# First attention of a two-block network in pairs of heads: row groups, column groups, one instruction for bias and maximum

## The chip, the cores and the metric

The kernel runs on one core of a Trainium2 chip. The metric is the device time of one execution in microseconds, the median of the runs shown. The core has a matrix engine (TensorE, PE in the rows, its weight loads PEld), a vector engine (DVE), an activation engine (ACT), GpSimd (POOL) and a sync engine (SP) that issues the weight transfers.

## The reference

Two transformer blocks in fp32 over 256 tokens of width 1024. The change touches the attention of the first block alone: eight sliding-window heads (window 128, two key/value heads, a learned sink per head) and eight heads that see all earlier tokens, each of width 64, each with a bias by distance.

```python
s = einsum(q, k) * HEAD_DIM ** -0.5 + bias          # masked: -inf
m = maximum(max(s), sink)                           # no sink in the second eight
p = exp(s - m); p = p / (sum(p) + exp(sink - m))
o = einsum(p, v)                                    # 64 columns per head
merged = sigmoid(ga) * (oa @ w_branch_a) + sigmoid(gb) * (ob @ w_branch_b)
```

The products with weights that surround it (`gate` = ga and gb, `bra` and `brb` = the two branches) use weights that arrive as fp32 and are split on the chip into a high part (`whi`) and a low part (`wlo`), so that each 128x128 tile takes three matmuls of 256 columns.

## The kernel before, in words

Each engine has its program written out by hand; the order in the source is the order on the engine, and semaphores tie them together. Weights come in chunks of 128 x 1024 (512 KB), in `raw`. For a chunk that is multiplied, ACT writes `whi` (L1138) and DVE writes `wlo` (L1518). For a chunk of the modulation weights (`ada`), DVE multiplies and adds two pieces of 512 columns (`ada_piece`, L1538 for a first part, L1541 for later ones, L1547 sums at the end of four). Scores of a head are fp32 matmuls, which the trace shows as two instructions each.

The stage of interest runs over `i = 0..17`. In step `i` TensorE does the scores of head `i` (`scores1`, L734 and L735, 64 rows of the array, into bank `A[i % 2]`), the 24 matmuls of `gate{i}` (L614 to L616), the three transposes of head `i-1` (L745) and the values of head `i-2` (`values1`, L759 and L760, 64 columns of the array, into `A[3]`). After steps 4, 8, 12 and 16 it also turns a modulation sum (`mod_sum`, L660).

DVE in step `i` does `shifts1(i)`: scaled score plus bias into `sc1` (L1680, L1681), two maxima (L1687, L1688), for heads with a sink the sink's maximum (L1691); then the `ada` piece of the step, the reciprocal (L1697 and L1699 with a sink, L1702 without), `splits(gate i)`, which is the low half of the chunk that `gate{i+1}` opens with (L1518), after odd steps the affine step that makes a sigmoid of the tanh (L1720), and the low half of a pair's output (L1728). ACT does the exponentials (L1257, L1258, L1260), the high half of a chunk that lies two gates ahead, the tanh (L1268), the copy of the transposed weights (L1275) and the high half of the output (L1279). GpSimd multiplies the exponentials by the reciprocal (L2129, L2130). `p1`, `sc1` and `pT1` hold two heads each.

The low half that `gate{i+1}` needs is thus made on DVE behind the shift, the `ada` piece and the reciprocal of head `i`, all of which wait for the scores of head `i`.

Of the kernel before, what the change touches and what calls it, by code (L numbers as in the profile page):

```python
# [14 lines left out]
P = 128  # L15
# [5 lines left out]
HD = 64  # L21
# [368 lines left out]
def build_program(nc, xT, metaT, vecs, consts, bands, bias_oh, bias_rows, wstream, scratch, outT):  # L390
# [6 lines left out]
    with ctx:  # L397
# [136 lines left out]
        ada_sets += [(flat(sc1[:, :, :])[:, 0:4 * P], flat(p1[:, :, :])[:, 0:4 * P])]  # L534
# [55 lines left out]
        def tensor_program(e):  # L590
# [146 lines left out]
            def transposes1(i):
# [5 lines left out]
                for j in range(3):  # L743
                    to = (j + 1) % 3
                    m = e.transpose(A[2][:, to * P:(to + 1) * P], p1[:, i % 2, j * P:(j + 1) * P], ident)  # L745
                m.then_inc(transposed1, 1)

            def values1(i):
                h, b, half = heads[i], i % 2, i % 2
                vv = lambda kt: vtok[:, kt, h["v"]:h["v"] + HD]  # L750
                o = A[3][half * HD:(half + 1) * HD, :]
                if i == 0:
# [3 lines left out]
                elif not half:  # L756
                    e.wait_ge(o_lo, i // 2)
                e.wait_ge(pT1_done, i + 1)
                e.matmul(o[:, 0:SEQ], vv(0), pT1[:, b, 0:SEQ], start=True, stop=False, skip_group_check=True)  # L759
                e.matmul(o[:, P:SEQ], vv(1), pT1[:, b, SEQ:384], start=False, stop=True, skip_group_check=True).then_inc(valued1, 1)  # L760
# [9 lines left out]
            for i in range(HEADS1 + 2):  # L770
                if i < HEADS1:
                    scores1(i)
                    if i % 2 == 0:
                        gate_out = pair(f"gate{i}")
                    gemm(f"gate{i}", [gate_out[:, t, 0:SEQ] for t in range(2)], src1, k0=4 * (i % 2), ktotal=KT)
                else:
                    branch_a(i - HEADS1)
                if 1 <= i <= HEADS1:
                    transposes1(i - 1)
                if i >= 2:  # L780
                    values1(i - 2)
                if i in HEAD_MODS:
                    mod_sum(HEAD_MODS[i], int(HEAD_MODS[i][3:]))
# [343 lines left out]
        def scalar_program(e):  # L1127
# [103 lines left out]
            def qk_copy(i):  # L1231
# [6 lines left out]
                e.activation(dst, ps[:, :, :, ::-1] if 1 <= ts[0] <= 4 or ts[0] >= 9 else ps, ACT.Copy).then_inc(qk_act, 1)  # L1238
# [13 lines left out]
            def exps1(i):  # L1252
                h, b, st = heads[i], i % 2, stat[:, i % 4, :]
# [1006 lines left out]
```

## Time and profile before

| | |
|---|---|
| median of 3 runs | 1271.12 us (1270.24 to 1271.15) |
| the profiled execution | 1270.07 us, its span 1268.5 us |
| mean granted TensorE clock | 0.997 |
| busy: PE, PEld, DVE, ACT, POOL | 97%, 95%, 69%, 50%, 14% of the span |
| the stage of the change | from 79.5 us (first scores) to about 170.5 us (last values) |

A busy PE is modelled from pipelined matmuls; the distance from one start to the next tells more than a duration. Idle time is shown in square brackets with what ended it.

### The profile page before, as it was taken

The page shows a single profiled execution, that of the slowest core. Times are in us where ns is not written, and L with a number is a line of the kernel's source. Part 1 is how long each engine was busy: PE and PEld are TensorE (multiplying, and loading weights), DVE is VectorE, ACT ScalarE, POOL GpSimd, SP SyncE. Part 2 cuts the span into 40 slices and gives each one's busy share as a digit, 9 for nine tenths or more (in the row PEclk, how much of TensorE's full clock was granted, in tenths as well). Part 3 has the DMA queues.
Part 4 walks back from the last instruction along what each step waited for, and adds up shares of the span by engine and source line. Part 5 has one row for each costly group of instructions (what it writes and reads, how often), then busy time and mean ns, then how long its engine had stood idle before and what let it go on. Part 6 is the DMA issues. An engine that isn't in the chain of part 4 may idle for free.

```text
span 1268.5 us, 23765 instructions
## 1 busy us (share of the span) xinstructions
PE 1230.6 (97%) x9924; PEld 1202.7 (95%) x9924; DVE 879.5 (69%) x1239; ACT 633.5 (50%) x986; POOL 177.8 (14%) x177
## 2 busy tenths in 40 slices
PE   4999999999999999999999999999999999999997
PEld 3998899999999999999899999999999997999997
DVE  7789889877566766655666666666666786766654
ACT  5545545766444444543544444445444466545531
POOL 2015424000132000012200001220000231000021
PEclk9999999999999999999999999999999999999999
DMA  8976564666655555555355555455656532655650
GB/s 325 324 305 207 203 250 161 242 248 248 212 158 166 178 186 168 180 170 181 100 175 184 174 185 166 166 173 192 196 178 208 183 116 68 215 181 186 190 160 34
DMA packets 67570, 239.16 MB, mean 189 GB/s; under 512 B 7366, under 2 KB 9592, under 8 KB 67464
## 3 DMA queue, kind: packets, MB, share of 16 engines
q1 hardware_dynamic: 66872, 235.46, 55.3%
q0 software_dynamic: 592, 2.19, 0.5%
q8 instruction: 78, 1.28, 0.4%
q14 instruction: 28, 0.23, 0.1%
HBM read 236.55 MB, written 1.07 MB: 187 GB/s over the span
## 4 chain that ended last, share of the span: by engine, by line
PE 87%; DVE 6%; ACT 1%; issue 1%; POOL 1%; DVEq 0%; ACTq 0%
PE G L614 26%; PE G L615 26%; PE G L616 26%; DVE sb_wlo L1518 2%; PE A L759 1%; PE A L734 1%; PE A L614 1%; PE A L615 1%; PE A L616 1%; DVE sb_xl L2044 0%; DVE sb_hidf L1607 0%; ACT sb_whi L1138 0%; PE A L745 0%; DVE sb_xl L1583 0%; PE A L1027 0%
## 5 line engine op out<-in xcount | busy, mean ns | idle before, releaser
L1518 DVE TENSOR_TENSOR sb_wlo<-sb_raw,sb_whi 128x1024 fp32r<-128x1024 f32 (+1 forms) x398 | 485.9, 1254 | 80.8 <-ACT sb_whi L1138 80.5
L614 PE MATMUL G<-sb_xh,sb_whi 128*128 128x256 f32 (+2 forms) x1752 | 497.9, 284 | 5.0 <-DVE sb_wlo L1518 2.2
L615 PE MATMUL G<-sb_xl,sb_whi 128*128 128x256 f32 (+2 forms) x1752 | 497.8, 284 | 0.0
L616 PE MATMUL G<-sb_xh,sb_wlo 128*128 128x256 f32 (+2 forms) x1752 | 496.3, 283 | 0.0
L1138 ACT ACTIVATE sb_whi<-sb_raw 128x1024 fp32r<-128x1024 f32 (+1 forms) x398 | 405.0, 1043 | 182.9 <-PE G L616 166.3
L614 PEld LDWEIGHTS G<-sb_xh,sb_whi 128*128 128x128 f32 x1752 | 330.7, 189 | 8.3 <-DVE sb_gu L1846 2.6
L616 PEld LDWEIGHTS G<-sb_xh,sb_wlo 128*128 128x128 f32 x1752 | 330.4, 189 | 0.0
L615 PEld LDWEIGHTS G<-sb_xl,sb_whi 128*128 128x128 f32 x1752 | 330.0, 188 | 0.0
L614 PE MATMUL G<-sb_hh,sb_whi 128*128 128x256 f32 (+1 forms) x1056 | 299.1, 283 | 0.7 <-DVE sb_hh L1738 0.7
L616 PE MATMUL G<-sb_hh,sb_wlo 128*128 128x256 f32 (+1 forms) x1056 | 298.2, 282 | 0.0
L615 PE MATMUL G<-sb_hl,sb_whi 128*128 128x256 f32 (+1 forms) x992 | 280.4, 283 | 0.0
L614 PEld LDWEIGHTS G<-sb_hh,sb_whi 128*128 128x128 f32 x1056 | 198.6, 188 | 1.1 <-issue 0.6
L616 PEld LDWEIGHTS G<-sb_hh,sb_wlo 128*128 128x128 f32 x1056 | 198.6, 188 | 0.0
L615 PEld LDWEIGHTS G<-sb_hl,sb_whi 128*128 128x128 f32 x992 | 186.7, 188 | 0.0
L1364 ACT ACTIVATE sb_gu<-sb_gu 128x272 f32<-128x272 f32 (+1 forms) x88 | 37.4, 425 | 191.6 <-DVE sb_gu L1846 191.3
L1846 DVE TENSOR_TENSOR sb_gu<-G,sb_rstd 128x544 f32<-128x544 f32 (+1 forms) x84 | 59.4, 707 | 60.1 <-PE G L616 60.1
L2086 POOL TENSOR_TENSOR sb_sumsq<-sb_X 128x256 f32<-128x256 f32 (+1 forms) x6 | 3.7, 622 | 651.5 <-DVE sb_X L1576 651.5
L1852 DVE TENSOR_TENSOR sb_hidf<-sb_gu 128x272 f32<-128x272 f32 (+1 forms) x88 | 38.2, 434 | 50.1 <-ACT sb_gu L1364 50.1
L1855 DVE TENSOR_TENSOR sb_hl<-sb_hidf,sb_hh 128x272 fp32r<-128x272 f32 (+1 forms) x88 | 38.1, 434 | 43.2 <-ACT sb_hh L1366 43.2
L1366 ACT ACTIVATE sb_hh<-sb_hidf 128x272 fp32r<-128x272 f32 (+1 forms) x88 | 37.4, 425 | 50.6 <-DVE sb_hidf L1852 50.6
L2091 POOL TENSOR_TENSOR sb_sq<-sb_X 128x256 f32<-128x256 f32 (+1 forms) x41 | 31.5, 767 | 203.7 <-DVE sb_X L1576 203.7
L1576 DVE SCALAR_TENSOR_TENSOR sb_X<-G,sb_X 128x272 f32<-128x272 f32 (+1 forms) x32 | 12.4, 427 | 48.0 <-PE G L616 48.0
(328 smaller groups left out, 1301.2 us busy)
## 6 DMA issues: line engine op xcount, KB each, us to landing
sb_raw<-in_wstream SPq DMA_DIRECT2D x438, 512.0 KB, 4.4
sb_raw<-in_wstream SPq DMA_DIRECT2D x8, 320.0 KB, 6.4
sb_bias<-bias_scratch POOLq DMA_DIRECT2D x1, 2048.0 KB, 16.0
sb_X<-in_xT SPq DMA_DIRECT2D x2, 512.0 KB, 6.4
out_T<-sb_X SPq DMA_DIRECT2D x4, 256.0 KB, 2.7
sb_con<-in_consts SPq DMA_DIRECT2D x1, 601.0 KB, 7.8
sb_band<-in_bands SPq DMA_DIRECT2D x1, 314.0 KB, 4.8
sb_vec<-in_vecs SPq DMA_DIRECT2D x1, 82.5 KB, 2.0
```

The lines of the kernel that those rows point to most:

```text
L614: e.matmul(out, w_h, xs, start=k0 + s.kt == 0, stop=False)
L615: e.matmul(out, w_h, xr, start=False, stop=False)
L616: m = e.matmul(out, w_l, xs, start=False, stop=k0 + s.kt == ktotal - 1)
L734: e.matmul(bank[:, 0:SEQ], q(1), k(SEQ), start=True, stop=True)
L1138: e.activation(whi[:, i % NSPLIT, 0:w], raw[:, c % NRAW, 0:w], ACT.Copy).then_inc(hi_done, 1)
L1364: e.activation(gu[:, b, 0, 0:n], gu[:, b, 0, 0:n], ACT.Silu).then_inc(silu_done, 1)
L1366: e.activation(hh[:, j * n:(j + 1) * n], hidf[:, b, 0:n], ACT.Copy).then_inc(hid_hi, 1)
L1518: e.tensor_tensor(wlo[:, i % NSPLIT, 0:w], raw[:, c % NRAW, 0:w], f(whi[:, i % NSPLIT, 0:w]), ALU.subtract).then_inc(lo_done, 1)
L1846: e.tensor_tensor(gu[:, b, :, 0:n], G[plan.pair[name]][:, :, 0:n], rb, ALU.mult).then_inc(left_dve, 1)
L1852: e.tensor_tensor(hidf[:, b, 0:n], gu[:, b, 0, 0:n], gu[:, b, 1, 0:n], ALU.mult).then_inc(hid_mul, 1)
L1855: e.tensor_tensor(hl[:, sl], hidf[:, b, 0:n], f(hh[:, sl]), ALU.subtract).then_inc(hid_lo, 1)
L2091: e.tensor_tensor(s, src, src, ALU.mult).then_inc(sumsq_done, 1)
```

## The change

- TensorE: the stage runs over pairs `p` of heads (rows 0 to 63 and 64 to 127 of the array, banks `A[0]` and `A[1]`). The scores of a pair stand together, head by head in turn; then the transposes of head `2p-2`, `gate{2p}`, the modulation sum, the transposes of head `2p-1`, `gate{2p+1}`, and the values of the earlier pair, again in turn, in column groups 0 to 63 and 64 to 127.
- DVE: bias, sign and minimum in one `tensor_tensor_reduce` per part (it writes the negative of score plus bias into `p1` and the negative maximum, clamped by the sink, into `stat`). Both heads of a pair are shifted before the first `ada` piece. The scale of 1/8 moves to the copies of the queries. `sc1` is gone, `p1` holds four heads, and the exponential works in place with scale -1.
- The sigmoid's affine step is gone: `(tanh + 1)` is multiplied in where the branch is gated, and the factor 0.5 goes into the copy of the attention's output.

```diff
-            def scores1(i):
+            def scores1(p):
+                pairs = [(heads[2 * p + n], A[n]) for n in range(2)]
...
+                for h, bank in pairs:
+                    e.matmul(bank[:, 0:SEQ], q(h, 1), k(h, SEQ), start=True, stop=True)
+                for h, bank in pairs:
+                    e.matmul(bank[:, SEQ:SEQ + P], q(h, 0), k(h, P), start=True, stop=True).then_inc(scored1, 1)
...
+                e.wait_ge(pT1_done, 2 * p + 2)
+                for n in range(2):
+                    e.matmul(o(n)[:, 0:SEQ], vv(n, 0), pT1[:, n, 0:SEQ], start=True, stop=False, skip_group_check=True)
+                for n in range(2):
+                    m = e.matmul(o(n)[:, P:SEQ], vv(n, 1), pT1[:, n, SEQ:384], start=False, stop=True, skip_group_check=True)
+                m.then_inc(valued1, 1)
...
+            for p in range(HEADS1 // 2 + 1):
+                if p < HEADS1 // 2:
+                    scores1(p)
+                    gate_out = pair(f"gate{2 * p}")
+                if p:
+                    transposes1(2 * p - 2)
+                if p < HEADS1 // 2:
+                    gate_src(2 * p)
+                else:
+                    branch_a(0)
+                if 2 * p in HEAD_MODS:
+                    mod_sum(HEAD_MODS[2 * p], int(HEAD_MODS[2 * p][3:]))
+                if p:
+                    transposes1(2 * p - 1)
+                if p < HEADS1 // 2:
+                    gate_src(2 * p + 1)
+                else:
+                    branch_a(1)
+                if p:
+                    values1(p - 1)
...
-                e.activation(p1[:, b, 0:SEQ], sc1[:, b, 0:SEQ], ACT.Exp, bias=st[:, 0:1], accum_out=st[:, 2:3])
+                e.activation(w[:, 0:SEQ], w[:, 0:SEQ], ACT.Exp, bias=st[:, 0:1], scale=-1.0, accum_out=st[:, 2:3])
...
-                e.scalar_tensor_tensor(sc1[:, b, 0:SEQ], bank[:, 0:SEQ], HD ** -0.5, bias[:, h["bias"], :], ALU.mult, ALU.add)
-                e.tensor_reduce(md[:, 0:1], sc1[:, b, 0:SEQ], AX_X, ALU.max, negate=neg)
+                e.tensor_tensor_reduce(w[:, 0:SEQ], bank[:, 0:SEQ], bias[:, h["bias"], :], -1.0, least, ALU.add, ALU.min, st[:, 0:1])
+                e.tensor_tensor_reduce(w[:, SEQ:384], bank[:, SEQ:384], bias[:, h["bias"], P:SEQ], -1.0, least, ALU.add, ALU.min, st[:, 1:2]).then_inc(sc1_done, 1)
...
+                    shifts1(2 * p)
+                    shifts1(2 * p + 1)
+                    if p:
+                        ada_piece(*ADA_HEADS[2 * p])
+                    recip1(2 * p)
+                    splits(f"gate{2 * p}")
+                    recip1(2 * p + 1)
...
+                    ada_piece(*ADA_HEADS[2 * p + 1])
+                    splits(f"gate{2 * p + 1}")
...
-                        e.tensor_scalar(d, d, 0.5, 0.5, ALU.mult, ALU.add).then_inc(sig_done, 1)
+                e.scalar_tensor_tensor(dst, sig[:, t:t + 2, :], 1.0, G[plan.pair[name]][:, :, 0:SEQ], ALU.add, ALU.mult).then_inc(left_dve, 1)
```

On TensorE before, between two gates, for a head in mid-stage (`A2` takes transposes, `A3` values, `A0` and `A1` scores):

```order
L616 MATMUL G1<-sb_xh,sb_wlo 128x256
L745 MATMUL A2<-sb_con,sb_p1 128x128 [waits weighted1,pT1_done]
L745 MATMUL A2<-sb_con,sb_p1 128x128 x2
L759 MATMUL A3<-sb_pT1,sb_vtok 64x256 [waits pT1_done]
L760 MATMUL A3<-sb_pT1,sb_vtok 64x128
L734 MATMUL A0<-sb_qk 128x256 [waits sc1_done]
L735 MATMUL A0<-sb_qk 128x128
```

The same place after the change, between the two gates that enclose a pair's beginning (line numbers are the changed kernel's):

```order
L763 MATMUL A3<-sb_pT1,sb_vtok 64x256 [waits pT1_done,o_lo]
L763 MATMUL A3<-sb_pT1,sb_vtok 64x256
L765 MATMUL A3<-sb_pT1,sb_vtok 64x128 x2
L736 MATMUL A0<-sb_qk 128x256 [waits sc1_done]
L736 MATMUL A1<-sb_qk 128x256
L738 MATMUL A0<-sb_qk 128x128
L738 MATMUL A1<-sb_qk 128x128
L748 MATMUL A2<-sb_con,sb_p1 128x128 [waits weighted1,pT1_done,left_act]
L748 MATMUL A2<-sb_con,sb_p1 128x128 x2
```

Values and scores of two heads stand side by side, and one head's transposes moved behind the scores; the other head's stand between the two gates.

On DVE before, the work of one head with a sink, up to the low half of the next gate's chunk:

```order
L1680 SCALAR_TENSOR_TENSOR sb_sc1<-A1,sb_bias 128x256
L1681 SCALAR_TENSOR_TENSOR sb_sc1<-A1,sb_bias 128x128
L1687 TENSOR_REDUCE sb_stat<-sb_sc1 128x1
L1688 TENSOR_REDUCE sb_stat<-sb_sc1 128x1
L1691 TENSOR_SCALAR sb_stat<-sb_stat,sb_vec 128x2
L1541 SCALAR_TENSOR_TENSOR sb_gu<-sb_raw,sb_csil,sb_gu 128x512 x2
L1697 TENSOR_TENSOR sb_stat<-sb_stat 128x2
L1699 RECIPROCAL sb_stat<-sb_stat 128x2
L1518 TENSOR_TENSOR sb_wlo<-sb_raw,sb_whi 128x1024
```

The same place after, for a pair with sinks; each `ISA` row with `sb_p1` is a `tensor_tensor_reduce`, the row of one column behind it reads its result out:

```order
L1716 ISA sb_p1,sb_stat<-A0,sb_bias,sb_neg_sinks 128x256 [waits transposed1,scored1]
L1716 ISA sb_stat 128x1
L1717 ISA sb_p1,sb_stat<-A0,sb_bias,sb_neg_sinks 128x128
L1717 ISA sb_stat 128x1
L1716 ISA sb_p1,sb_stat<-A1,sb_bias,sb_neg_sinks 128x256 [waits transposed1,scored1]
L1716 ISA sb_stat 128x1
L1717 ISA sb_p1,sb_stat<-A1,sb_bias,sb_neg_sinks 128x128
L1717 ISA sb_stat 128x1
L1569 SCALAR_TENSOR_TENSOR sb_gu<-sb_raw,sb_csil,sb_gu 128x512 [waits ada_acc,loaded5]
L1569 SCALAR_TENSOR_TENSOR sb_gu<-sb_raw,sb_csil,sb_gu 128x512 [waits ada_acc]
L1723 TENSOR_TENSOR sb_stat<-sb_stat 128x2 [waits sink_done]
L1725 RECIPROCAL sb_stat<-sb_stat 128x2 [waits den_done]
```

Behind these rows comes the low half of the chunk of `gate{2p+1}` (L1546). The shifts of a second head now stand ahead of it.

## Rows read from the trace of the kernel before

**Rows 1.** The page's first part: busy time and share of each engine.
```profile
PE 1230.6 (97%) x9924; PEld 1202.7 (95%) x9924; DVE 879.5 (69%) x1239; ACT 633.5 (50%) x986; POOL 177.8 (14%) x177
```
**Rows 2.** Windows: stretch, length, PE, PEld, DVE, ACT, POOL busy, clock, DMA share, GB/s.
```profile
95.60:115.60 20.00, 19.84 (x142) 17.24 (x141) 18.20 (x47) 10.47 (x32) 9.15 (x8) 1.00 0.60 209
```
**Rows 3.** Timeline of PE, one head's round: start, length, engine, line, what.
```profile
95.63 0.70 PE L734 MATMUL A<-sb_qk 64*128 64x256 f32 x2
...
96.48 0.39 PE L614 MATMUL G<-sb_xh,sb_whi 128*128 128x256 f32 x1
...
96.94 0.28 PE L614 MATMUL G<-sb_xh,sb_whi 128*128 128x256 f32 x1
...
99.41 0.49 PE L745 MATMUL A<-sb_con,sb_p 128*128 128x128 f32 x3
99.83 0.65 PE L759 MATMUL A<-sb_pT,sb_vtok 128*64 128x256 f32 x2
...
100.63 0.70 PE L734 MATMUL A<-sb_qk 64*128 64x256 f32 x2
```
**Rows 4.** Timeline of PE: the modulation sum of a round that has one.
```profile
105.81 0.66 PE L660 MATMUL G<-sb_con,sb_hidf 128*128 128x128 f32 x4
106.40 0.70 PE L734 MATMUL A<-sb_qk 64*128 64x256 f32 x2
```
**Rows 5.** Timeline of PE in the second attention: values of two heads.
```profile
1056.90 0.66 PE L1065 MATMUL A<-sb_pT,sb_v 128*64 128x256 f32 x4
1057.38 0.40 PE L1066 MATMUL A<-sb_pT,sb_v 128*64 128x128 f32 x4
1057.71 0.48 PE L1061 MATMUL A<-sb_pT,sb_v_meta 32*128 32x128 f32 x2
```
**Rows 6.** Timeline of DVE, heads without a sink, from the shift to the split.
```profile
133.11 0.43 DVE L1680 SCALAR_TENSOR_TENSOR sb_sc<-A,sb_bias 128x256 f32<-128x256 f32 x1
...
133.77 0.42 DVE L1687 TENSOR_REDUCE sb_stat<-sb_sc 128x1 f32<-128x256 f32 x1
...
134.30 1.40 DVE L1541 SCALAR_TENSOR_TENSOR sb_hidf<-sb_raw,sb_csil,sb_hidf 128x512 f32<-128x512 f32 x2
...
135.70 1.20 DVE L1518 TENSOR_TENSOR sb_wlo<-sb_raw,sb_whi 128x1024 fp32r<-128x1024 f32 x1
...
144.39 0.87 DVE L1538 TENSOR_SCALAR sb_gu<-sb_raw,sb_csil 128x512 f32<-128x512 f32 x2
```
**Rows 7.** Timeline of DVE: the shift that waited for the scores of 95.63 us.
```profile
96.59 0.42 DVE L1680 SCALAR_TENSOR_TENSOR sb_sc<-A,sb_bias 128x256 f32<-128x256 f32 x1 [0.73 <-PE A L735]
```
**Rows 8.** Timeline of DVE: `ada` pieces, denominator of a sink head, the split.
```profile
93.05 1.41 DVE L1541 SCALAR_TENSOR_TENSOR sb_hidf<-sb_raw,sb_csil,sb_hidf 128x512 f32<-128x512 f32 x2
94.38 0.16 DVE L1697 TENSOR_TENSOR sb_stat<-sb_stat 128x2 f32<-128x2 f32 x1
...
94.66 1.21 DVE L1518 TENSOR_TENSOR sb_wlo<-sb_raw,sb_whi 128x1024 fp32r<-128x1024 f32 x1
```
**Rows 9.** Lines, 79 to 160 us: count, busy us, mean ns of one.
```profile
L1257 ACT ACTIVATION_READ_ACCUMULATOR sb_p<-sb_sc,sb_stat 128x1 f32 x15 | 2.8, 187 | 0.0
```
**Rows 10.** Timeline: the first head's exponentials and the split behind them on ACT.
```profile
82.32 0.51 ACT L1257 ACTIVATE sb_p<-sb_sc,sb_stat 128x256 f32<-128x256 f32 x1 [2.41 <-DVE sb_stat L1691]
...
83.40 1.99 ACT L1138 ACTIVATE sb_whi<-sb_raw 128x1024 fp32r<-128x1024 f32 x2
```
**Rows 11.** Timeline of PE: the second gate begins late, and ends.
```profile
85.75 0.39 PE L614 MATMUL G<-sb_xh,sb_whi 128*128 128x256 f32 x1 [1.50 <-DVE sb_wlo L1518]
...
90.22 0.50 PE L745 MATMUL A<-sb_con,sb_p 128*128 128x128 f32 x3
```
**Rows 12.** Windows behind the late gate, columns as in rows 2.
```profile
86.50:87.00 0.50, 0.50 (x5) 0.50 (x4) 0.46 (x3) 0.00 (x0) 0.00 (x0) 0.50 0.02 8
```
**Rows 13.** Timeline of PE: another idle stretch, in the second attention.
```profile
1056.49 0.48 PE L1061 MATMUL A<-sb_pT,sb_v_meta 32*128 32x128 f32 x2 [1.18 <-DVE sb_o2l L2036]
```
**Rows 14.** The window behind that stretch, columns as in rows 2.
```profile
1057.00:1058.00 1.00, 1.00 (x10) 0.69 (x10) 0.79 (x4) 0.90 (x1) 0.00 (x0) 1.00 0.00 0
```

More of the change, by code:

```diff
@@ L755, in values1 @@
                     e.wait_ge(left_dve, plan.left_dve["v"])
[L756 to L760, printed above, removed]
+                else:
+                    e.wait_ge(o_lo, p)
+                e.wait_ge(pT1_done, 2 * p + 2)
[4 more added lines that the diff above has]
+                m.then_inc(valued1, 1)
             def branch_a(i):
@@ L1252, in exps1 @@
             def exps1(i):
[L1253 to L1258 removed]
+                h, w, st = heads[i], p1[:, i % 4, :], stat[:, i % 4, :]
@@ L1259, in exps1 @@
+                e.wait_ge(sc1_done, i + 1)
+                e.activation(w[:, 0:SEQ], w[:, 0:SEQ], ACT.Exp, bias=st[:, 0:1], scale=-1.0, accum_out=st[:, 2:3])
+                e.activation(w[:, SEQ:384], w[:, SEQ:384], ACT.Exp, bias=st[:, 1:2], scale=-1.0, accum_out=st[:, 3:4]).then_inc(exp1_done, 1)
                 if h["sink"] is not None:
                     e.activation(st[:, 4:6], st[:, 0:2], ACT.Exp, bias=V("sinks", h["sink"])).then_inc(sink_done, 1)
[L1262 to L1279 removed]
@@ new lines, in scalar_program @@
+            for p in range(HEADS1 // 2 + 1):
+                if p >= 2:
+                    output_high(p - 2)
+                if p:
+                    turned1(2 * p - 2)
+                if p < HEADS1 // 2:
+                    exps1(2 * p)
+                    exps1(2 * p + 1)
+                    splits(f"gate{2 * p}")
+                else:
+                    splits("bra0")
+                if p:
+                    turned1(2 * p - 1)
+                if p < HEADS1 // 2:
+                    splits(f"gate{2 * p + 1}")
+                    e.wait_ge(mm_done, ended[f"gate{2 * p + 1}"])
+                    e.activation(sig[:, 2 * p:2 * p + 2, :], G[plan.pair[f"gate{2 * p}"]][:, :, 0:SEQ], ACT.Tanh, scale=0.5).then_inc(left_act, 1)
+                else:
+                    splits("bra1")
@@ L1670, in vector_program @@
             mod_out("mod4")
+            e.tensor_scalar(neg_sinks[:, :], V("sinks", 0, SWA_HEADS), -1.0, None, ALU.mult).then_inc(sinks_set, 1)
             def shifts1(i):
-                h, b, bank, st = heads[i], i % 2, A[i % 2], stat[:, i % 4, :]
+                h, w, bank, st = heads[i], p1[:, i % 4, :], A[i % 2], stat[:, i % 4, :]
                 e.wait_ge(scored1, i + 1)
@@ new lines, in vector_program @@
+            branch_a = lambda i: gated(sig[:, 2 * i:2 * i + 2, :], f"bra{i}", 2 * i, 2 * i)
+            for p in range(HEADS1 // 2 + 1):
+                if p < HEADS1 // 2:
+                    shifts1(2 * p)
+                    shifts1(2 * p + 1)
+                    if p:
+                        ada_piece(*ADA_HEADS[2 * p])
+                    recip1(2 * p)
+                    splits(f"gate{2 * p}")
+                    recip1(2 * p + 1)
+                else:
+                    splits("bra0")
+                    branch_a(0)
+                if p >= 2:
+                    output_low(p - 2)
+                if 2 * p in HEAD_MODS:
+                    mod_out(HEAD_MODS[2 * p])
+                if p < HEADS1 // 2:
+                    ada_piece(*ADA_HEADS[2 * p + 1])
+                    splits(f"gate{2 * p + 1}")
+                else:
+                    splits("bra1")
+                    branch_a(1)
```

148 lines of the change are left out of this document (51 added, 97 removed).

## The prediction

> **What bounds the kernel now.** I read the page first: TensorE is busy for 97% of the span and DVE for 69% [rows 1]. Such shares are means over stages, so I went to the stage that is changed and asked for its windows. From 95.6 to 115.6 us TensorE is busy for 19.84 of 20 us at full clock, and DVE for 18.20 [rows 2]. TensorE sets the pace, but DVE is only 8% behind. Whatever makes TensorE shorter here must be looked at on DVE too.
>
> Then the timeline of TensorE, one round [rows 3]: scores 95.63 to 96.48 (0.85 us), gate 96.48 to 99.41 (2.93), transposes 99.41 to 99.83 (0.42), values 99.83 to 100.63 (0.80). Together 5.0 us, and the next scores start at 100.63, 5.00 after the last. A round with a modulation sum has 0.59 more [rows 4]. Sixteen heads, so eight pairs of 10.0 us each. In the steady rounds there is next to no waiting.
>
> **TensorE, part by part.** *Values in column groups.* The trace of before has this very thing in the second attention: there the values of two heads, eight instructions of the same shapes, in two column groups, go from 1056.90 to 1057.71, so 0.81 us for two heads [rows 5], against 0.80 for one here. So a pair costs 0.81 and saves 0.79.
>
> *Scores in row groups.* No row shows two row groups side by side. Bounds: 0.85 for the pair if they overlap as the column groups do, and 1.60 if they run one after the other (twice 0.85 less one change of array shape). I take 0.85, because the nearest thing in the trace is the pair of column groups [rows 5]: a 64-wide operand, the same fp32 pairs of instructions, a separate half of the array, a separate place for the result.
>
> The Trainium skill ("TensorE: Matmul & The Clock Gate", Part 3, Measured speedup vs the span model) reports that four row groups of 32 gave 3.07 times the throughput, not 4. An estimate from that page, with the same loss for two groups, puts a pair's scores at 1.3 times 0.85, 1.1 us, which would take some 1.8 us off the gain over seven pairs. No run shown here tells it; the term above does not use it.
>
> *Changes of array shape.* The first gate matmul after scores is 0.39 long and a later one 0.28 [rows 3], 0.11 for the change of shape. Before, a pair has six such changes, two of which go with the removed scores and values; three remain after, since both gates now stand next to transposes. One more is saved, 0.11.
>
> So TensorE needs 10.0 - 0.85 - 0.79 - 0.11 = 8.25 us for a pair, plus 0.59 in every second one. The gate's 48 matmuls and the six transposes of a pair stay.
>
> **DVE, part by part.** Of a head without sink it now spends 133.11 to 133.77 on score plus bias (0.66), 133.77 to 134.30 on the maxima (0.53), 134.30 to 135.70 on the `ada` pieces and the reciprocal (1.40), and 1.20 on the split [rows 6]. The change makes the first two into one instruction per part, each with a read-out of one column behind it. No row has this instruction. Bounds for a pair of heads (384 columns each): 1.3 us if it costs what score plus bias costs alone (twice 0.66), 2.4 if the maxima cost as before (twice 1.19). If it ran at half the rate of a plain one, 2.8. A read-out costs between 0.07 (the reciprocal's slot before the split: 1.40 [rows 6] less 1.33 for the pieces, 93.05 to 94.38 [rows 8]) and 0.19 (the same kind of instruction on ACT [rows 9]); four of them give 1.6 to 2.1. I take 1.6, since a tiny DVE instruction behind another is the nearer row. The affine step on the tanh goes too, which DVE spends nothing on any more; the gating instruction keeps its size.
>
> All in all DVE's load stays below TensorE's 8.25: 1.6 + 1.33 + 1.33 + two splits of 1.2 + about 0.9 for reciprocals and the output's low half + 0.8 for a modulation step or an `ada` sum, so 8.0 to 8.4 per pair with sinks. That is close. But the load isn't what I expect to decide; the order is.
>
> **The wait that the change adds.** `gate{2p+1}` opens a chunk whose low half DVE makes behind *both* shifts, the `ada` pieces and the reciprocal of head `2p`. Before, one shift stood ahead of it, and TensorE had a gate, transposes, values and the next scores to do meanwhile. Count from the start of the pair's scores:
> - DVE begins the shifts at 0.96 (scores at 95.63 [rows 3], shift at 96.59 [rows 7]); shifts 1.6; `ada` and reciprocal 1.40 without a sink [rows 6] and 1.33 + 0.28 with one (94.38 to 94.66 [rows 8]); split 1.20; about 0.05 until TensorE starts. Ready at 5.2, or 5.4 with a sink.
> - TensorE gets there after scores 0.85, transposes 0.42, gate 2.83 (2.93 less most of the 0.11 for the change of shape, which now falls on the transposes), transposes 0.35 (no change of shape on either side): at 4.45.
> - So it waits 0.76 without and 0.96 with a sink. Behind it on TensorE stand the whole gate, the values and the next scores, so the wait is paid in full.
> - In the even pairs (2, 4, 6) the modulation sum adds 0.59 on TensorE, and the `ada` pieces are first parts, 0.87 instead of 1.40 [rows 6], 0.53 less on DVE: ready at 4.9 at most, wanted at 5.04. No wait.
> Pairs 1 and 3 (sinks) and 5 and 7 (none) give 2 x 0.96 + 2 x 0.76 = 3.4 us.
>
> The other chains have room. The second split of a pair is done some 8.5 to 9.2 after the pair's start and wanted at about 10.2. ACT's turned weights of head `2p-1` are ready at about 5.6 for values at about 8.1. The output's low half of an earlier pair is made in mid-pair. GpSimd's two products per pair, 2.5 us each (9.15 us for about four heads [rows 2]), fit into 8.8. DMA moves 209 GB/s at a share of 0.60 [rows 2]; the same bytes in 12% less time ask for about 240.
>
> **The first pair is a case of its own.** Before, `gate1` began at 85.75 after 1.50 us of idle time [rows 11], because ACT did the high half behind the exponentials of head 0 (82.32 to 83.40, 1.08 us [rows 10]). Behind it the granted clock is 0.50, so 1.2 GHz [rows 12], and the gate took 4.47 us (85.75 to 90.22 [rows 11]) instead of 2.85: 1.62 lost. After the change two heads' exponentials stand there, 1.08 more, less some 0.65 that the shorter shift gives back: the gate begins 0.4 later, at about 86.2. The saved scores vanish in that wait. The first transposes, done before at 90.22, still have to be done. I put the pair at a loss of 0.45, with the same clock loss as before.
>
> **The sum.** Seven pairs (1 to 7) at 10.0 - 8.25 = 1.75: 12.25. The last pair's values, half of them saved: 0.79. First pair: -0.45. Makes 12.6. Less the waits of 3.4: 9.2 us. Against the profiled execution 1270.07 (span 1268.5 and 1.6 around it) that is 1260.9; the median stands 1.05 above it, so I forecast 1271.1 - 9.2 = **1261.9 us**.
>
> **The rivals.**
> 1. *Waits smaller than I say.* If the new instruction costs 1.3 per pair, or DVE comes to the shifts earlier, the waits fall to 2.3 or to nothing: 1260.8, at best 1258.5. For it: DVE's instructions follow each other tightly [rows 6]. Against: DVE cannot start before the scores, and the chain of 0.96 + 1.3 + 1.40 + 1.25 is 4.9 even so. If also the first pair's clock did not fall, 1257.
> 2. *Row groups don't overlap; this part of the change doesn't do what it says.* Seven pairs at 0.75 more (the first is hidden in its wait) cost 5.25, and the waits shrink to some 2.8 since DVE starts only 0.6 later: gain 4.6, 1266.5. Against it: the column groups did overlap [rows 5]. For it: results of row groups go through all 128 output partitions at once, which the column groups don't.
> 3. *DVE takes over, and the clock falls: slower.* One mechanism: the wait ahead of the odd gates reaches the length after which the clock halved at 85.75, 1.50 us [rows 11, 12]; 1.18 us did not do it, the clock stood at 1.00 behind it [rows 13, 14]. Each fall costs 1.62. With a read-out of 0.19 (2.1 per pair) the odd waits are 1.46 and 1.26 and the even ones 0.65 together, in all 6.1, each still short of it: 1264.6. With 2.4 per pair they are 1.77 and 1.56 in the odd pairs and 1.5 together in the even: 12.6 - 8.2 - 4 x 1.62 = -2.1, so 1273.2. At half rate, 2.8 per pair, 12.6 - 11.0 - 6.5 = -4.9: 1276.0. It decides from about 2.35 us per pair. For it: bias and maximum in one instruction may be two passes. Against: one operand comes from PSUM in both forms, and today's form with two tensor operands takes 0.43 for 256 columns where the maximum with one takes 0.42 [rows 6].
>
> On the third, the Trainium skill ("TensorEngine Tiling (Array Packing)", Performance Considerations, PSUM Bottleneck) warns that tiling speeds up TensorE but not the evacuation of PSUM, which can then become the bound. It names the mechanism of rival 3 and gives no figure for it. By the windows [rows 2] and the sum above the load would just fit; that the evacuation of two heads stands in one piece ahead of the split is what makes its warning bite here.
>
> **How the numbers follow.** Forecast and its neighbours (1259.5 to 1264.5): 0.55. Rival 1 below that: 0.14. Rival 2 and mixed cases (1264.5 to 1268.5): 0.18. No change within 0.2% (2.5 us, about what a measurement of this kernel can tell from none): 0.06. Slower, rival 3: 0.07. The range goes from 1257 to 1267: it takes in rival 1 whole and rival 2, and leaves out the rest, about 0.15 to 0.2.
>
> **What would show it.** In the new profile: L736 (scores) to the transposes in 0.85 to 0.9 per pair, against 1.6 under rival 2; L763 to L736 in 0.8; the pair of shifts on DVE in 1.6, against 2.4 or more; PE waiting for `sb_wlo` ahead of `gate3`, `7`, `11` and `15` for 0.7 to 1.0 each and not ahead of the even ones; a fall of the clock only in the first pair; pairs of 9.0 to 9.2 (odd) and 8.8 (even). The forecast is wrong if a long wait stands at a place that I called roomy (the transposes waiting for GpSimd, ACT's queue with both exponentials ahead of a split), or if later stages wait for data and give the gain back.

## The result, and the profile after

The changed kernel takes 1260.72 us (median of 4 runs, 1259.29 to 1262.37) where the kernel before took 1270.69 beside it (4 runs, 1270.24 to 1271.15). The ratio is 0.9919, with a 95% interval of 0.9906 to 0.9931: 10.3 us faster, between 8.8 and 11.9 (the two medians are 10.0 apart). The forecast was 1261.9. The profiled execution of the changed kernel took 1260.69, its span is 1259.3, against 1270.07 and 1268.5 before.

The page's first part answers to [rows 1]. DVE has 12 us less to do, TensorE is as full as before.

```profile
PE 1219.0 (97%) x9924; PEld 1196.1 (95%) x9924; DVE 867.5 (69%) x1224; ACT 634.8 (50%) x986; POOL 178.1 (14%) x177
```

The same stretch of time as [rows 2], by windows, with the same columns. TensorE's share fell from 19.84 to 18.74 of 20 us, and yet it got through 160 matmuls instead of 142. DVE stands at 17.78, GpSimd at 13.06 instead of 9.15, and the transfers at 244 GB/s instead of 209.

```profile
95.60:115.60 20.00, 18.74 (x160) 17.21 (x160) 17.78 (x46) 13.70 (x35) 13.06 (x11) 1.00 0.70 244
```

The timeline of TensorE answers to [rows 3, 4]: start, length, line, what, and in brackets the idle time with its releaser. It shows pair 1 from its scores on, and pair 2 up to the next scores; left out are the gate's matmuls.

```profile
91.11 0.70 PE L736 MATMUL A<-sb_qk 64*128 64x256 f32 x4
...
91.96 0.55 PE L748 MATMUL A<-sb_con,sb_p 128*128 128x128 f32 x3
92.26 0.36 PE L615 MATMUL G<-sb_xh,sb_whi 128*128 128x256 f32 x1
...
95.17 0.49 PE L748 MATMUL A<-sb_con,sb_p 128*128 128x128 f32 x3
96.28 0.39 PE L615 MATMUL G<-sb_xh,sb_whi 128*128 128x256 f32 x1 [0.62 <-DVE sb_wlo L1546]
...
99.29 0.65 PE L763 MATMUL A<-sb_pT,sb_vtok 128*64 128x256 f32 x4
...
100.09 0.70 PE L736 MATMUL A<-sb_qk 64*128 64x256 f32 x4
...
104.15 0.60 PE L661 MATMUL G<-sb_con,sb_hidf 128*128 128x128 f32 x4
104.58 0.49 PE L748 MATMUL A<-sb_con,sb_p 128*128 128x128 f32 x3
104.83 0.36 PE L615 MATMUL G<-sb_xh,sb_whi 128*128 128x256 f32 x1
...
108.63 0.70 PE L736 MATMUL A<-sb_qk 64*128 64x256 f32 x4
```

Read the starts. Scores of two heads: 91.11 to 91.96, 0.85. Values of two heads: 99.29 to 100.09, 0.80. Pair 1 is 8.98 long and has a wait ahead of `gate3`; pair 2 is 8.54 and has none, although it turns a modulation sum (104.15 to 104.58, 0.43). Without a wait the gate starts 0.25 behind the transposes (104.58 to 104.83), with it 1.11 (95.17 to 96.28). So the wait is worth 0.86, more than the 0.62 in the bracket, because the bracket counts from the modelled end of the transposes. Pairs 3 and 5, by the same view (pair 7 is like 5, 0.69 from 147.31 to 148.00):

```profile
112.69 0.49 PE L748 MATMUL A<-sb_con,sb_p 128*128 128x128 f32 x3
113.81 0.38 PE L615 MATMUL G<-sb_xh,sb_whi 128*128 128x256 f32 x1 [0.64 <-DVE sb_wlo L1546]
...
130.21 0.49 PE L748 MATMUL A<-sb_con,sb_p 128*128 128x128 f32 x3
130.89 0.39 PE L615 MATMUL G<-sb_xh,sb_whi 128*128 128x256 f32 x1 [0.19 <-DVE sb_wlo L1546]
```

By the same subtraction the waits are 0.86, 0.87, 0.43 and 0.44, together 2.6 us; forecast were 3.4. The timeline of DVE shows why:

```profile
92.06 0.48 DVE L1716 CUSTOM_DVE_ANT_0 sb_p<-A,sb_bias,sb_neg_sinks 128x256 f32<-128x256 f32 x1 [2.61 <-PE A L738]
92.47 0.08 DVE L1716 DVE_READ_ACCUMULATOR2_ANT sb_stat<- 128x1 f32 x1
92.47 0.35 DVE L1717 CUSTOM_DVE_ANT_0 sb_p<-A,sb_bias,sb_neg_sinks 128x128 f32<-128x128 f32 x1
...
93.42 1.41 DVE L1569 SCALAR_TENSOR_TENSOR sb_hidf<-sb_raw,sb_csil,sb_hidf 128x512 f32<-128x512 f32 x2
...
95.02 1.20 DVE L1546 TENSOR_TENSOR sb_wlo<-sb_raw,sb_whi 128x1024 fp32r<-128x1024 f32 x1
...
118.58 0.42 DVE L1716 CUSTOM_DVE_ANT_0 sb_p<-A,sb_bias 128x256 f32<-128x256 f32 x1 [0.76 <-PE A L738]
...
119.69 0.88 DVE L1566 TENSOR_SCALAR sb_hidf<-sb_raw,sb_csil 128x512 f32<-128x512 f32 x2
```

The read-out and the next instruction start at the same time (92.47): the read-out costs nothing. The four instructions of a pair take 1.36 with sinks (92.06 to 93.42), and 1.11 without (118.58 to 119.69); the 256-column one is 0.48 long where the sink is its scalar and 0.42 where a constant is, the length of today's score plus bias alone [rows 6].

**The first pair**, answering to [rows 10 to 12]. TensorE, the first shift on DVE, and ACT ahead of the gate:

```profile
86.55 0.58 PE L615 MATMUL G<-sb_xh,sb_whi 128*128 128x256 f32 x1 [2.98 <-DVE sb_wlo L1546]
```
```profile
81.25 0.48 DVE L1716 CUSTOM_DVE_ANT_0 sb_p<-A,sb_bias,sb_neg_sinks 128x256 f32<-128x256 f32 x1 [0.18 <-DVE sb_neg_sinks L1704]
```
```profile
82.05 0.51 ACT L1271 ACTIVATE sb_p<-sb_p,sb_stat 128x256 f32<-128x256 f32 x1 [1.98 <-DVE sb_stat L1717]
...
84.19 1.99 ACT L1151 ACTIVATE sb_whi<-sb_raw 128x1024 fp32r<-128x1024 f32 x2
```

The gate begins at 86.55 (forecast 86.2) after 2.98 us of idle time, and by the windows, with the columns of [rows 2], the granted clock behind it is 0.50 (1.2 GHz), as in [rows 12]:

```profile
86.60:90.00 3.40, 3.40 (x16) 3.40 (x17) 2.85 (x4) 0.53 (x1) 2.98 (x2) 0.50 0.22 35
```

**Where the time went.** I compared when the same matmul, numbered from 0 in order of start on TensorE, starts in both traces. The 1180th stands a few microseconds behind the stage, at 184.47 before and 173.34 after: 11.1 us gained. The 9900th stands near the end, at 1256.11 and 1246.85: 9.3 left. So 1.8 us are given back after the stage, in three places where the gated hidden layer is multiplied (`hh` and `hl`): matmuls 2150 to 2900 take 87.59 us before and 88.38 after, 7200 to 7850 75.94 and 76.39, 9250 to 9923 80.09 and 80.68. There is no idle time there; each of these 256-column matmuls follows the last by 117.78 ns instead of 116.67. The windows show it as one matmul less in 15 us, before:

```profile
335.00:350.00 15.00, 15.00 (x131) 1.00 0.76 246
```

and after (stretch, length, PE busy with its count, clock, DMA share, GB/s):

```profile
335.00:350.00 15.00, 15.00 (x130) 1.00 0.42 129
```

These matmuls are no part of the change. What the change does to them is that `neg_sinks`, 32 bytes in each partition, is allocated ahead of `hh` and `hl` and moves them up by 32 bytes.

### The profile page after: what moved, and what is told of

It is laid out like the page before. It is cut to its first block, busy times and chain, and to the rows that moved or that the text cites. A ratio compares the mean times of both kernels' runs of the same rounds, so it can differ in the third digit from the quotient of the medians.

```text
span 1259.3 us, 23727 instructions
## 1 busy us (share of the span) xinstructions
PE 1219.0 (97%) x9924; PEld 1196.1 (95%) x9924; DVE 867.5 (69%) x1224; ACT 634.8 (50%) x986; POOL 178.1 (14%) x177
## 4 chain that ended last, share of the span: by engine, by line
PE 88%; DVE 6%; ACT 1%; issue 1%; POOL 0%; DVEq 0%; ACTq 0%
PE G L616 26%; PE G L615 26%; PE G L617 26%; DVE sb_wlo L1546 2%; PE A L615 1%; PE A L616 1%; PE A L617 1%; DVE sb_xl L2077 0%; DVE sb_hidf L1635 0%; ACT sb_whi L1151 0%; PE A L763 0%; PE A L736 0%; DVE sb_xl L1611 0%; PE A L1040 0%; PE G L1095 0%
## 5 line engine op out<-in xcount | busy, mean ns | idle before, releaser
L1546 DVE TENSOR_TENSOR sb_wlo<-sb_raw,sb_whi 128x1024 fp32r<-128x1024 f32 (+1 forms) x398 | 486.6, 1257 | 82.8 <-ACT sb_whi L1151 82.5
L615 PEld LDWEIGHTS G<-sb_xh,sb_whi 128*128 128x128 f32 x1752 | 330.5, 189 | 10.3 <-DVE sb_wlo L1546 5.8
```

Source lines behind the costliest of these rows:

```text
L615: e.matmul(out, w_h, xs, start=k0 + s.kt == 0, stop=False)
L1546: e.tensor_tensor(wlo[:, i % NSPLIT, 0:w], raw[:, c % NRAW, 0:w], f(whi[:, i % NSPLIT, 0:w]), ALU.subtract).then_inc(lo_done, 1)
```

## The experiments

Questions: do row and column groups really carry the gain (e1, e2)? What gives 1.8 us back behind the stage (e3, e4)? Do the waits cost what I say and come from DVE's order (e5)? Would the slower shift have taken the gain (rival 3, e6), and what is each half of the change worth alone (e6, e7)? Is the first pair's loss ACT's queue (e8)? e1 to e4 shared one chip (before: 1269.45, 17 runs), e5 to e8 another (before: 1270.0, 21 runs). The changed kernel itself did not run beside them, so times are set against the ratio to before, and what a single edit does is read from the traces.

### e1_same_rows: scores of both heads from one row group

```diff
-                pairs = [(heads[2 * p + n], A[n]) for n in range(2)]
+                pairs = [(heads[2 * p], A[n]) for n in range(2)]
```

> The changed kernel, with one edit: the second head of each pair takes its scores from the first head's queries and keys, so that both stand in one row group; the scores of every second head are thus the first head's. Nothing else is edited. Theory (row groups run at the same time, and that is half of the gain): from the first score matmul of a pair to its first transpose 1.6 us in place of 0.85, seven pairs 0.75 later each, the waits ahead of the odd gates some 0.3 us smaller in all since the shifts begin later: 1260.7 + 5 = 1265.5 us. Rival (the gain comes from the shorter DVE work and the saved changes of shape, the row groups run one after the other anyway): 0.85 stays and so does 1260.7.

Measured: 1261.28 (one run, span 1259.9), against 1265.5 by the theory and 1260.7 by the rival. The timeline of TensorE, pair 1 to the next scores:

```profile
89.71 1.13 PE L736 MATMUL A<-sb_qk 64*128 64x256 f32 x4
...
91.21 0.55 PE L748 MATMUL A<-sb_con,sb_p 128*128 128x128 f32 x3
...
95.31 0.39 PE L615 MATMUL G<-sb_xh,sb_whi 128*128 128x256 f32 x1 [0.41 <-DVE sb_wlo L1546]
...
99.11 1.13 PE L736 MATMUL A<-sb_qk 64*128 64x256 f32 x4
```

In one row group the pair's scores take 1.50 (89.71 to 91.21), so two groups side by side save 0.65 of it, all that there is to save; pair 1 is 9.40 instead of 8.98, since the wait shrinks from 0.62 to 0.41. The theory's row is confirmed (1.6 expected) and the rival's 0.85 is not, although the total lies nearer to the rival's. It does so for two reasons of its own. The second gate of the first pair waited 2.33 us, and the clock did *not* fall behind it:

```profile
86.70:89.70 3.00, 3.00 (x24) 2.87 (x24) 2.85 (x4) 0.55 (x1) 2.72 (x2) 1.00 0.04 11
```

24 matmuls in 3.00 us, where the changed kernel took 4.56 (86.55 to 91.11). And the `hh` matmuls came faster in part: 86.93 us for numbers 2150 to 2900. Even so the 1180th matmul starts at 175.58, 2.24 later than in the changed kernel, with 1.5 of clock loss spared: 3.8. The rows give the same: seven times 0.65, less 0.8 by which the waits shrink, plus 0.1 in the first pair, 3.8. The one total was no measure of the term.

### e2_same_cols: values of both heads into one column group

```diff
-                o = lambda n: A[3][n * HD:(n + 1) * HD, :]
+                o = lambda n: A[3][0:HD, :]
```

> The changed kernel, with one edit: both heads of a pair write their values to the column group 0 to 63 of the array, so that the second head's overwrite the first's. Theory: values of a pair 1.58 us in place of 0.80, eight pairs 0.78 later each: 1260.7 + 6.2 = 1266.9 us. The rival (no overlap of column groups) would leave 0.80 and 1260.7.

Measured: 1264.12 (one run, span 1262.7), against 1266.9 by the theory and 1260.7 by the rival. The timeline of TensorE:

```profile
99.51 1.08 PE L763 MATMUL A<-sb_pT,sb_vtok 128*64 128x256 f32 x4
...
100.95 0.70 PE L736 MATMUL A<-sb_qk 64*128 64x256 f32 x4
```

The pair's values take 1.44 instead of 0.80 (1.58 was expected), eight times: 5.1 us. The 1180th matmul starts at 178.45 instead of 173.34, 5.1 later, of which 0.2 was there at the second gate (86.74 against 86.55). The clock fell in the first pair as in the changed kernel. Behind the stage numbers 2150 to 2900 took 86.93 us instead of 88.38, so 1.4 came back, and 1260.7 + 5.1 - 1.4 is 1264.4.

### e3_sinks_last: the same tile, allocated behind the others

```diff
-        neg_sinks = sb("neg_sinks", [P, SWA_HEADS])
...
+        neg_sinks = sb("neg_sinks", [P, SWA_HEADS])
```

> The changed kernel, with the new 32 byte wide tile neg_sinks allocated last in place of ahead of the hidden tiles, so that hh, hl and all behind them lie at the addresses of the kernel before. Same instructions. In the two profiles 11.2 us are gained by the end of the attention and 9.2 are left at the end; the pace of matmuls that read hh and hl with 256 columns went from 116.67 to 117.78 ns, while those that read xh, which did not move, kept 116.95. Theory A (the address of the streamed operand sets that pace): pace back to 116.7, some 1.6 us less in all, 1259.1. Theory B (the pace differs by run or chip, not by address): as the changed kernel, 1260.7, with 117.8 or any other pace.

Measured: 1259.05 (6 runs, 1257.18 to 1262.02), ratio to before 0.9916 [0.9903, 0.9929]. The windows show before's count again:

```profile
335.00:350.00 15.00, 15.00 (x131) 1.00 0.47 132
```

The three stretches take 87.59, 75.94 and 80.09 us, to the hundredth what they took before. In the allocation `xh`, `xl`, `whi` and `wlo` lie ahead of the new tile and did not move, so it is the place of `hh` and `hl` that sets the pace, and no wait or transfer does. The profiled span is 1257.6, 1.7 shorter. In the medians the two kernels' intervals overlap: the mechanism is shown in the traces, its 1.8 us are not shown in the times.

### e4_before_pad: the kernel before, with an unused tile of 32 bytes

```diff
+        unused = sb("unused", [P, SWA_HEADS])
```

> The kernel before, with an unused tile 32 bytes wide ahead of qsc, which moves hh, hl and all behind them by 32 bytes, as the change does. Same instructions. Theory A (address): pace of the matmuls on hh and hl with 256 columns from 116.67 to 117.8 ns, 1.6 us more: 1272.3, ratio 1.0013. Theory B (run or chip): 1270.7, ratio 1.000.

Measured: 1270.42 (12 runs), ratio 1.0004 [0.9995, 1.0013]. Theory A asked for 1.0013 and B for 1.000; the interval holds both, and the move alone makes no difference that can be measured. The windows say why, two neighbouring stretches:

```profile
335.00:350.00 15.00, 15.00 (x130) 1.00 0.79 241
350.00:365.00 15.00, 15.00 (x134) 1.00 0.48 162
```

At the moved place the pace is 117.78 ns at first (130 in 15 us), and in this trace it is *faster* later on, 113.3 ns (134). The stretch from 2150 to 2900 takes 86.93 us here, less than before; the other two take 76.40 and 80.67. Together that is 0.4 us more than before where theory A had 1.6. Of the six traces with the moved place, four (e1, e2, e4, e6) have the fast second part in this stretch, and two (the changed kernel and e5) have not (88.38). The four traces with the old place (before, e3, e7, e8) all take 87.59 there. What decides it at the moved place is open.

### e5_split_first: the low half right behind the shifts

```diff
                     shifts1(2 * p + 1)
+                    splits(f"gate{2 * p}")
                     if p:
                         ada_piece(*ADA_HEADS[2 * p])
                     recip1(2 * p)
-                    splits(f"gate{2 * p}")
```

> The changed kernel, with one edit on DVE: within a pair the low half for the next gate is made right behind the two shifts, ahead of the ada pieces and of both denominators. Same instructions. In the changed kernel's trace the second gate of pairs 1, 3, 5 and 7 begins 1.11, 1.12, 0.68 and 0.69 us after the transposes ahead of it, where 0.33 is enough. Theory (the wait is the position of the split behind two shifts and the ada pieces): the split is ready at 0.96 + 1.36 + 1.25 = 3.6 us after the pair's start, wanted at 4.45, all four waits gone, 2.3 us less: 1258.4, or ratio to before 0.990. Rival (the wait is ACT's high half behind four exponentials, or GpSimd): waits stay, 1260.7.

Measured: 1258.17 (5 runs, 1256.88 to 1260.36), ratio 0.9904 [0.9891, 0.9918]. That is the theory's number (0.990). The list of TensorE's waits from 79 to 182 us (engine, line, what it waited for: us in total, times, longest), of the changed kernel:

```profile
PE G L615 <- DVE sb_wlo L1546: 4.6, 5, 3.0
```

and of this one:

```profile
PE G L615 <- DVE sb_wlo L1546: 3.0, 1, 3.0
...
PE A L748 <- POOL sb_p L2163: 0.4, 1, 0.4
PE A L763 <- DVE sb_ol L1734: 0.4, 1, 0.4
```

Four of five waits are gone, and pair 1 takes 8.10 (89.23 to 97.33), against 8.98. What is next late takes 0.8, once each near the end of the stage (146.85 and 148.16). The 1180th matmul starts at 169.54, 3.8 earlier. Of it 0.3 was there when the second gate began, and 1.5 is the clock, which did not fall in the first pair of this trace in spite of the same 2.98 us of idle time:

```profile
86.22 0.38 PE L615 MATMUL G<-sb_xh,sb_whi 128*128 128x256 f32 x1 [2.98 <-DVE sb_wlo L1546]
```
```profile
86.30:89.10 2.80, 2.80 (x24) 2.79 (x24) 2.77 (x6) 0.50 (x1) 2.56 (x3) 1.00 0.00 0
```

That leaves 2.0 for the waits, where the rows have 2.6 less the 0.8 that comes in their place. The waits are thus DVE's order, not its load.

### e6_old_shift: pairs of heads, with the shift in two steps as before

```diff
-                e.tensor_tensor_reduce(w[:, 0:SEQ], bank[:, 0:SEQ], bias[:, h["bias"], :], -1.0, least, ALU.add, ALU.min, st[:, 0:1])
+                e.scalar_tensor_tensor(w[:, 0:SEQ], bank[:, 0:SEQ], -1.0, bias[:, h["bias"], :], ALU.mult, ALU.subtract)
...
+                e.tensor_reduce(md[:, 0:1], w[:, 0:SEQ], AX_X, ALU.min)
```

> The changed kernel with the shift as it was: score plus bias, then the extremum by a reduction, then for sinks the clamp, in place of the one instruction per part; pairs and all else as changed. Theory (DVE's time for a pair of shifts sits on the path, 1.1 to 1.36 us now, 2.4 to 2.7 then): 1.3 more ahead of each of the four odd gates and 0.9 to 1.1 ahead of the three even ones, 8.1 us more: 1268.8, ratio 0.998. If in addition the granted clock falls behind waits of 1.5 us and more, as it did behind the first gate, 1.6 more for each: up to 1275. Rival (TensorE's pairing is the whole gain and DVE has room): 1260.7.

Measured: 1271.01 (10 runs, 1268.09 to 1272.47), ratio 1.0005 [0.9996, 1.0015], between the 1268.8 of the theory and the 1275 with a fall of the clock behind every long wait. The whole gain is gone. DVE's timeline has the two heads' shifts from 94.32 to 97.20, 2.88 us. TensorE's waits, by the list for the same stretch, and the second and third of them in the timeline:

```profile
PE G L616 <- DVE sb_wlo L1547: 13.3, 8, 4.1
```
```profile
100.05 0.58 PE L616 MATMUL G<-sb_xh,sb_whi 128*128 128x256 f32 x1 [2.14 <-DVE sb_wlo L1547]
...
111.57 0.39 PE L616 MATMUL G<-sb_xh,sb_whi 128*128 128x256 f32 x1 [1.17 <-DVE sb_wlo L1547]
```

Even pairs wait too now. By the windows the clock stood at half through the whole second gate of the first pair, fell again behind the 2.14 us at 100.05, and did not fall behind another 2.14 us, at 122.06:

```profile
88.10:93.20 5.10, 5.10 (x24) 5.10 (x24) 2.82 (x4) 0.49 (x1) 2.99 (x2) 0.50 0.47 149
100.10:103.50 3.40, 3.40 (x16) 3.40 (x17) 3.36 (x5) 0.67 (x1) 3.40 (x4) 0.50 0.91 325
122.10:125.00 2.90, 2.90 (x24) 2.86 (x24) 2.86 (x6) 0.67 (x1) 2.90 (x3) 1.00 0.82 328
```

The 1180th matmul starts at 185.54, 12.2 later than in the changed kernel: 2.3 of it stands at the end of the first pair (93.37 against 91.11), some 1.5 is the second fall, and the 8.4 left are near the 8.1 that the theory had for the waits.

### e7_unpaired: the kernel before with DVE's part of the change alone

Heads one by one as before; bias and minimum in one instruction, and the sigmoid's step folded in. `neg_sinks` stands behind the other tiles. The shift of a head:

```diff
-                e.scalar_tensor_tensor(sc1[:, b, 0:SEQ], bank[:, 0:SEQ], HD ** -0.5, bias[:, h["bias"], :], ALU.mult, ALU.add)
...
-                e.tensor_reduce(md[:, 0:1], sc1[:, b, 0:SEQ], AX_X, ALU.max, negate=neg)
...
+                e.tensor_tensor_reduce(sc1[:, b, 0:SEQ], bank[:, 0:SEQ], bias[:, h["bias"], :], -1.0, least, ALU.add, ALU.min, st[:, 0:1])
```

> The kernel before with the DVE part of the change alone: one instruction for bias and extremum, the scale in the copies of the queries, no affine step on the tanh; TensorE's order, single heads, as before; the new tile lies last, so that all others keep their addresses. Theory (TensorE sets 5.0 us a head and DVE only fills behind it): 0.5 us from the shorter first wait and 0.3 from the small ones, 1269.8, ratio 0.9993. Rival (the DVE work was what held the stage): 5 us or more less, below 1265.

Measured: 1268.38 (10 runs), ratio 0.9988 [0.9979, 0.9997]; the theory had 0.9993, the rival less than 1265 us. DVE's saving brings TensorE nothing in the steady rounds: by the timeline the scores of two heads in a row start at 93.92 and 98.91, still 5.0 apart. The 1180th matmul starts at 182.36, 2.1 us earlier than before. Of that 1.7 is in the first pair: the wait there is 1.08 instead of 1.50, with no fall of the clock behind it in this trace. The other 0.4 is two short waits of before in rounds with a modulation sum (a round took 5.77 from 100.63 to 106.40 [rows 3, 4], and takes 5.58 here).

```profile
85.56 0.38 PE L615 MATMUL G<-sb_xh,sb_whi 128*128 128x256 f32 x1 [1.08 <-DVE sb_wlo L1522]
```

### e8_early_split: e3 and e5 together, and ACT's high half ahead of the first exponentials

```diff
+            split_hi(steps["gate0"][0].i + 1)
```

(in ACT's program ahead of the first exponentials, beside the edits of e3 and e5).

> Three edits together on the changed kernel: the split right behind the shifts (as in the run before), neg_sinks allocated last, and on ACT the high half of gate1's chunk ahead of the first exponentials. Theory: the wait ahead of gate1, 2.98 us, falls to about 0.5, and the clock has no reason to fall behind it (1.6 us where it fell); four odd waits gone (2.3); pace of the hidden tiles' matmuls 116.7 ns (up to 2.0): 1260.7 - 2.5 - 1.6 - 2.3 - 2.0 = 1252.3, ratio 0.9855. Rival (chunk 44 isn't there yet at 80 us, ACT waits for its DMA and the exponentials behind it): no gain in the first pair, 1256.4.

Measured: 1253.79 (4 runs, 1252.45 to 1254.5), ratio 0.9867 [0.9854, 0.9881]: faster than both kernels, the interval lies wholly below that of the change; the theory had 0.9855. The edits were made together, so their shares are not separated here. The timeline of ACT, and of TensorE behind it:

```profile
80.14 1.06 ACT L1151 ACTIVATE sb_whi<-sb_raw 128x1024 fp32r<-128x1024 f32 x1
82.24 0.51 ACT L1272 ACTIVATE sb_p<-sb_p,sb_stat 128x256 f32<-128x256 f32 x1 [1.03 <-DVE sb_stat L1718]
```
```profile
84.07 0.39 PE L615 MATMUL G<-sb_xh,sb_whi 128*128 128x256 f32 x1 [0.31 <-DVE sb_wlo L1547]
```

The high half of the first wanted chunk is made while ACT would otherwise wait for the shift. The wait of 2.98 becomes 0.31, the clock stays at 1.00 in the first pair, and the 1180th matmul starts at 167.27, 6.1 ahead of the changed kernel. In the profiled execution 1.5 of that goes again in the second attention, where the clock fell at 1041 us:

```profile
1039.52 0.48 PE L1074 MATMUL A<-sb_pT,sb_v_meta 32*128 32x128 f32 x2 [1.18 <-DVE sb_o2l L2070]
```
```profile
1041.20:1044.50 3.30, 3.30 (x17) 3.30 (x17) 2.08 (x3) 1.71 (x3) 0.00 (x0) 0.50 0.36 93
```

It is the same place and the same idle time as in [rows 13], behind which the clock of before stood at 1.00 [rows 14].

## Why the prediction was right, and where it was not

The forecast of a gain of 9.2 us met 10.3 (8.8 to 11.9), and the mechanisms are those that it named. Term by term:

- **Scores in row groups, 0.85 for a pair**: right, 0.85; alone in one group they take 1.50 (e1). The estimate from the Trainium skill ("TensorE: Matmul & The Clock Gate", Part 3, Measured speedup vs the span model), 1.1, is not borne out: two groups of 64 rows lost nothing here, 0.85 for two heads and 0.85 for one [rows 3].
- **Values, 0.81**: right, 0.80; in one group 1.44 (e2).
- **A pair of 8.25 without its sum and waits**: 8.10 (e5). The transposes between the gates take 0.25 instead of 0.35, the first ones 0.30 (91.96 to 92.26) instead of 0.42; the gate behind the first ones is 0.08 longer than I had it (2.91 against 2.83). My pair was 0.15 too long, seven times, 1.0 us.
- **The modulation sum, 0.59**: now 0.43. I carried the row of before over, though the sum's neighbour had changed from scores to transposes. Three times 0.16, 0.5; the fourth sum stood between values and a gate before and took 0.42 there already (166.85 to 167.27).
- **Waits of 3.4 in pairs 1, 3, 5 and 7, none in the even ones**: the right pairs, each, and 2.6 us. The term that was mis-sized is the pair of shifts, 1.6: it takes 1.36 with sinks and 1.11 without. Four read-outs at 0.07 are hidden whole, 0.28. The rest is that I took 0.66 for a head's two parts, up to the start of a maximum that had to wait for them [rows 6], where the second head now starts 0.56 behind the first. The sink costs 0.25 in each pair as the instruction's scalar, which I had not in the account; it is why the waits of pairs 5 and 7 came out 0.33 below the forecast and those of pairs 1 and 3 only 0.1, both after TensorE itself had come 0.15 sooner.
- **The first pair**: `gate1` at 86.55, forecast 86.2. I left out that the first shift waits for `neg_sinks`, an instruction of the change, and started the stage at before's time: the shift starts at 81.25, and at 80.75 before. The wait was 2.98 instead of 1.50. With the clock at half the gate took 4.56 where I had 4.47, so the pair ends 0.45 later than forecast.
- **"Next to no waiting" in the rounds of before**: two rounds with a sum were 0.17 and 0.19 longer than I priced them (5.77 from 100.63 to 106.40, against 5.0 + 0.59), and these short waits are gone too: 0.35 that the sum did not have.
- **Behind the stage nothing**: wrong. 1.8 us came back in `hh` and `hl` matmuls, the nearest of them 130 us behind the stage (e3).

With the measured terms the sum is 9.2 + 1.0 + 0.5 + 0.8 - 0.45 + 0.35 = 11.4 at the end of the stage, where the trace has 11.1; less the 1.8 of the later stretches that is 9.6, where the trace has 9.2 of span. Too cautious terms on TensorE and an unforeseen loss cancelled. That the total was nearer than its parts is luck.

**The rivals.** Rival 2 is refuted by the 0.85. Rival 1's waits of 2.3 came about (2.6), and its total of 1260.8 was the nearest of all, though for the reasons above only in part. Rival 3 did not happen, and e6 shows that its mechanism was real: what kept it away is the shorter shift. At 2.88 us for a pair of shifts, against a forecast bound of 2.8 with 1276.0, the kernel lands at 1271.0: 13.3 us of waits and a second fall of the clock. Against before that is 0.6 more where the rival had 4.9, so it was some 4 us too dark, since it had four more falls of the clock and one came, beside the longer first one.

Packing with the old shift (e6) gains nothing (1.0005), the faster shift alone (e7) 1.5 us (0.9988), and both 10.3. Neither half carries the gain; the one makes room on TensorE, and the other lets TensorE use it. It is what the Trainium skill ("TensorEngine Tiling (Array Packing)", Performance Considerations, PSUM Bottleneck) warns of, that tiling does not speed up the evacuation of PSUM, and these ratios agree with it. Both e6 and e7 hold the folded sigmoid and the moved scale, whose own share no run separates.

**The step that failed in kind** is the rule that I read out of [rows 11 to 14]: that the clock falls behind 1.50 us of idle time and not behind 1.18. It fell behind 1.18 (e8), and did not behind 1.72 (e4), 2.33 (e1), 2.98 (e5) or one of the two waits of 2.14 in e6. Behind the same wait of 2.98 it fell in the changed kernel and in e2, and not in e5. The length of one wait doesn't decide it; what does is not shown by these traces. Each fall costs 1.5 us (a gate of 4.56 instead of 3.0).

That clock loss is most of what makes executions of the kernel before differ. Of the 21 runs of before beside e5 to e8, the ten with a mean granted clock of 0.998 have a median of 1268.84 us, the seven with 0.997 one of 1270.41, and the two with 0.995 took 1272.21 and 1272.53. It is not all: in e4 two runs with 0.999 took 1270.53 and 1270.95. It also bears on e7. Four of its ten runs have 0.999, which before never reached, and the three at 0.998 have a median of 1268.17 against 1268.84: an estimate from these is that about half of e7's 1.5 us is the clock's.

**Left open**: what else decides a fall of the clock, and what sets the second pace (113.3 or 117.8) of the moved tiles.

## What to carry to other kernels

Where two small matmuls can share the array, look first at what stands ahead of the next thing that TensorE wants: if both heads' evacuation goes ahead of it, the saved time turns into a wait, and moving that one producer forward (on DVE behind the shifts, on ACT ahead of the exponentials), with the new tile out of the way, was worth another 6.6 us here (0.9919 to 0.9867, all three together). Add new small tiles behind the large ones: it costs nothing, though its worth here shows in the traces (1.8 us) and not in the times. Compare the pace of the same matmuls far from the edit, since a gain can be given back where nothing was changed. Price a wait by the distance of starts against a round that doesn't wait, and take the clock loss behind a wait as a chance, not as a threshold.

## What the runs showed of the hardware

- Two fp32 operands of 64 rows in two row groups cost what one costs: 0.85 us for the four score products of two heads (eight instructions), as for the two of one head before, against 1.50 in one group. Two results in two column groups: 0.80 against 1.44.
- The pace of 256-column matmuls on `hh` and `hl` depends on where these lie in SBUF: 116.67 ns at one place (before, e3), 117.78 ns 32 bytes further (the changed kernel, e4), and there, in four of six traces and part of the time, 113.3 ns.
- An instruction that adds and reduces in one (256 columns, one operand in PSUM) takes 0.42 us on DVE, as long as the addition alone; a scalar read from a tile makes it 0.48. Its read-out of 0.08 us starts together with the next instruction and costs nothing.
- Behind an idle stretch of 1.2 to 4.1 us the granted clock stood at 0.50 (1.2 GHz) in some executions (86.60 to 90.00 in the changed kernel; 88.10 to 93.20 in e6), and at 1.00 (2.4 GHz) throughout in others of the same stretch (e5).
